# One decoder trunk layer on one core: a wait dropped from SyncE, merge inputs in thirds, four output-weight buffers, experts' second rows in fp32

## The reference, cut to what matters

```python
z = layer_norm(x) @ w_in + b_in                 # queries, keys, values, gates of three token mixers
proj = einsum('blmc,mcd->blmd', branches, w_branch)       # three branches of 256 columns each
y = einsum('blmd,blmd->bld', sigmoid(gates), proj)        # merged by per-channel gates
x = layer_norm(alpha * x + y @ w_out)
h = silu(x @ w_gate[e]) * (x @ w_up[e]) * gate[e]         # 16 experts, each token goes to 2 of them
x = layer_norm(alpha * x + h @ w_down[e])
```

## Time and profile before

| | |
|---|---|
| three runs | 1563.55, 1564.02, 1569.73 us, median 1564.02 |
| the profiled execution | 1564.86 us, span of the trace 1562.8 us |
| PE matmul busy | 1392.9 us, 89% of the span |
| DVE, ACT, POOL busy | 612.7, 489.6, 301.1 us |
| DMA | 228.26 MB, mean 146 GB/s |

### The profile page before, as it was taken

How to read it: one execution, slowest core, us unless ns; L and a number is a source line. 1 busy time by engine, 2 the same in 40 slices (tenths; PEclk the granted TensorE clock), 3 DMA queues, 4 the chain that set the end, 5 groups by cost and what they waited for, 6 DMA issues and landing times. The chain is left out here.

```text
span 1562.8 us, 23344 instructions
## 1 busy us (share of the span) xinstructions
PE 1392.9 (89%) x8799; PEld 1183.2 (76%) x8799; DVE 612.7 (39%) x1598; ACT 489.6 (31%) x904; POOL 301.1 (19%) x406
## 2 busy tenths in 40 slices
PE   4899999999999999878889979969974999999945
PEld 3799999999888989845666646548854888888822
DVE  6122212222324223045676647844551333333317
ACT  4422222222122321136456544320012333333233
POOL 4311140020102000003343100001142222322203
PEclk9799999999999999869999989999986999999967
DMA  7135484163625234580004056732153788887745
GB/s 203 44 119 177 122 234 131 51 164 86 180 62 160 61 84 48 184 222 14 1 1 159 18 193 194 247 101 79 52 170 83 240 270 258 269 272 242 256 174 216
DMA packets 186943, 228.26 MB, mean 146 GB/s; under 512 B 47510, under 2 KB 154902, under 8 KB 185086
## 3 DMA queue, kind: packets, MB, share of 16 engines
q1 hardware_dynamic: 174254, 186.25, 39.0%
q0 software_dynamic: 12592, 40.71, 8.5%
HBM read 167.89 MB, written 60.19 MB: 146 GB/s over the span
## 5 line engine op out<-in xcount | busy, mean ns | idle before, releaser
L1251 PE MATMUL psum<-proj_x_hi,proj_w_hi 128*128 128x362 f32 (+1 forms) x1056 | 357.8, 339 | 8.2 <-DVE proj_w_lo L1373 6.4
L1251 PE MATMUL psum<-proj_x_lo,proj_w_hi 128*128 128x362 f32 (+1 forms) x1056 | 348.9, 330 | 0.0
L1251 PE MATMUL psum<-proj_x_hi,proj_w_lo 128*128 128x362 f32 (+1 forms) x1056 | 348.8, 330 | 0.0
L1251 PEld LDWEIGHTS psum<-proj_x_hi,proj_w_hi 128*128 128x128 f32 x1056 | 201.6, 191 | 13.8 <-DVE proj_w_lo L1373 6.7
L1251 PEld LDWEIGHTS psum<-proj_x_lo,proj_w_hi 128*128 128x128 f32 x1056 | 201.8, 191 | 0.0
L1251 PEld LDWEIGHTS psum<-proj_x_hi,proj_w_lo 128*128 128x128 f32 x1056 | 201.1, 190 | 0.0
L1373 DVE TENSOR_TENSOR proj_w_lo<-proj_w_raw,proj_w_hi 128x1024 fp32r<-128x1024 f32 x44 | 54.2, 1232 | 281.6 <-ACT proj_w_hi L1284 281.5
L1313 ACT ACTIVATE proj_sig<-psum,proj_bias 128x362 f32<-128x362 f32 (+1 forms) x72 | 40.5, 563 | 248.6 <-PE psum L1251 232.8
L2098 PE MATMUL psum<-branches_t,merge_branch_w 128*128 128x362 f32 (+1 forms) x288 | 90.2, 477 | 9.0 <-DMA branches_t<-branch_scratch 9.0
L2552 PE MATMUL psum<-moe_xgt,expert_gate_w 128*128 128x192 f32 x512 | 90.9, 332 | 0.7 <-ACT moe_xgt L2591 0.7
L2552 PEld LDWEIGHTS psum<-moe_xgt,expert_gate_w 128*128 128x128 f32 x512 | 86.8, 195 | 3.2 <-issue 1.1
(11 more groups left out here) (449 smaller groups left out, 2230.1 us busy)
## 6 DMA issues: line engine op xcount, KB each, us to landing
proj_w_raw<-in_w_in SPq DMA_DIRECT2D x43, 512.0 KB, 4.9
expert_gate_w<-in_moe_w_gate SPq DMA_DIRECT2D x16, 1024.0 KB, 9.0
expert_up_w<-in_moe_w_up SPq DMA_DIRECT2D x16, 1024.0 KB, 11.7
expert_down_w<-in_moe_w_down SPq DMA_DIRECT2D x16, 1024.0 KB, 13.6
merge_sig<-gate_scratch SPq DMA_DIRECT2D x24, 544.0 KB, 3.8
gate_scratch<-proj_sig SPq DMA_DIRECT2D x48, 181.0 KB, 1.9
final_pair<-expert_rows SPq DMA_DIRECT2D x8, 1024.0 KB, 11.9
feature_scratch<-proj_feat SPq DMA_DIRECT2D x13, 512.0 KB, 3.0
```

The source lines that it names most:

```text
L1251: mm = nc.tensor.matmul(k.ps[u % RING][:, 0:w], b[wt][:, x % 2, kk, :], b[xx][:, kk, a0:a0 + w], start=(kk == 0 and i == 0), stop=(kk == K ...
```

## The change

1. SP no longer waits for the side outputs at L374; it stores the gates and loads weight tiles on. POOL still waits for them.
2. Each of the three branches is read by three DMAs, one for each token chunk, the first of them ahead of the branch weight. PE waits for the chunk that it uses.
3. The raw buffers for `w_out` become four (`WRAW`). Four tiles are loaded in the merge, one behind the gates of each of the last four units; in the next stage SP has four left.
4. The experts' second 64 rows are four fp32 matmuls on the raw `w_down` and on `hid`, in place of 12 fp32r ones: output columns 0 to 511 go to partitions 0 to 63 of bank 6, columns 512 to 1023 to partitions 64 to 127 of it. ACT copies them in two pieces, `y1_done` counts two for an expert, and `w_down` may be overwritten only after the downs of the expert two before, no longer after its low part is made.

```diff
-        sp.wait_ge(s["side_out"], SIDE_OUT)
...
             for g in range(UNITS):
...
+                if g < 3:
+                    branch(g, 0)
                 sp.dma_start(b["branch_w"][:, g % RING], io["w_branch"][0, m].rearrange("(k p) n -> p k n", p=P)[:, :, dt * P:(dt + 1) * P]).then_inc(s[f"bw_loaded{g % RING}"], 16)
                 if g < 3:
-                    sp.dma_start(br_all[:, 2 * g:2 * g + 2, :], k.br_dram.rearrange("p (c t) -> p c t", c=6)[:, 2 * g:2 * g + 2, :]).then_inc(s[f"br_loaded{g}"], 16)
+                    branch(g, 1)
+                    branch(g, 2)
                 sp.dma_start(b["sig"][:, g % RING, :], k.sig_dram[g]).then_inc(s[f"sig_loaded{g % RING}"], 16)
-            for kk in range(2):
-                load_wo(k, sp, pre, ps, kk)
+                if g >= UNITS - WRAW:
+                    load_wo(k, sp, pre, ps, g - UNITS + WRAW)
...
-            for kk in range(2, KD):
-                sp.wait_ge(s["w_lo_done"], kk - 1)
+            for kk in range(WRAW, KD):
+                sp.wait_ge(s["w_lo_done"], kk - WRAW + 1)
                 load_wo(k, sp, pre, ps, kk)
...
-                        sp.wait_ge(s["wd_lo_done"], g + after("wd_lo_done", -1))
+                        sp.wait_ge(s["down_mm"], g * 2 + after("down_mm", -2))
                         load_down(k, sp, ew, ews, e, x)
...
+                pe.wait_ge(s["y1_done"], g * 2 + after("y1_done", 0))
+                for c in range(2):
                     for half in range(2):
-                        for c in range(2):
-                            for i, (hid, wd) in enumerate((("hid_hi", "wd_hi"), ("hid_lo", "wd_hi"), ("hid_hi", "wd_lo"))):
-                                mm = nc.tensor.matmul(k.ps[4 + 2 * j + half][0:n, :], b[hid][:, c, p0:p0 + n], b[wd][:, x, c, half * 512:(half + 1) * 512],
-                                                      start=(c == 0 and i == 0), stop=(c == 1 and i == 2))
-                    mm.then_inc(s["down_mm"], 1)
+                        mm = nc.tensor.matmul(k.ps[6][64 * half:64 * half + 64, :], b["hid"][:, c, P:CAP], ew["wd"][:, x, c, half * 512:(half + 1) * 512], start=(c == 0), stop=(c == 1))
+                mm.then_inc(s["down_mm"], 1)
...
-                nc.scalar.copy(b["y_out"][0:n, x, 1, :], k.psum[0:n, 6:8, :].rearrange("p b c -> p (b c)")).then_inc(s["y1_done"], 1)
+                for half in range(2):
+                    nc.scalar.copy(b["y_out"][0:n, x, 1, half * 512:(half + 1) * 512], k.ps[6][64 * half:64 * half + n, :]).then_inc(s["y1_done"], 1)
```

## The result

The changed kernel ran in 1540.46 us (median of four, 1538.97 to 1543.79), beside 1563.78 for the kernel before (four runs, 1557.57 to 1569.73). The ratio is 0.9856, interval 0.9831 to 0.9881: faster by 1.4%, 23 us of the 34.7 that were forecast. By the ratio the time is 0.9856 × 1564.02 = 1541.5, half a us above the upper end of the range. The direction was right and the size was not.

A forecast was written before the change was run, and what follows sets the result against it. PE, busy 89% of the span, was taken as the bound: time leaves only where it idles or works in a costlier form. 9.1 + 2.2 + 9.5 + 13.9 = 34.7 off 1564.86 gave 1530 us, range 1525 to 1541.

The forecast's parts named there:

- the halves overlap: Experts' second rows: column halves run side by side, 1.90 us a block; the no-overlap rival had 1555 us, 4%.
- the experts are not held by DMA: Experts: the rival had DMA failing to meet 275 GB/s, period staying 18.18, time 1544 us; 5%.
- `w_down` is not late: Experts: the rival had `w_down` landing 3.1 us late for 14 loads, 43 us lost, time 1573; 3%.
- the third rival: Projection's end: load of tile 42 waits behind the outputs, meets POOL's fetches, lands near 637; time 1539 us; 6%.
- Part 1 (9.1): Projection's end: without SP's wait, 6.38 us of idle PE and 2.72 of slow passes go; lower bound 4.4.
- it will be quicker: Projection's end: load of tile 42 meets a DMA share of 0.05, so lands faster than 11.0 us.
- Part 2 (2.2): Merge start: with branches in thirds PE begins at about 922.3 instead of 924.49; bounds 1.0 and 2.6.
- the last third may land up to a us late: Merge start: thirds issued half a us apart against 1.3 us a chunk on PE; gives the bounds 1.0 and 2.6.
- Part 3 (9.5): Mix: with four raw buffers kk 7 could begin at 1032.5 in place of 1042.36; bounds 8.0 and 9.8.
- Part 4 (13.9): Experts' second rows: 1.90 us in place of 2.77, 0.87 less for each of 16 experts; bounds 16.6 and −11.0.
- The staggered rival: Experts' second rows: passes start strictly in order, five slots, 2.21 us; gain 9.0, time 1535 us; 12%.
- goes against the profiled execution: Whole kernel: gains are subtracted from one profiled execution, 1564.86 us, 0.84 above the runs' median, without correction.

The follow-up runs named there:

- the three sets: Unaltered changed kernel against the kernel before, measured three times: 1540.46, 1533.29 and 1541.25 us, ratios 0.9856, 0.9821 and 0.9841.
- part 4 alone: Kernel before with only the experts' second rows changed to fp32 matmuls: 1554.54 us, ratio 0.9929.
- part 2 alone: Kernel before with only the branches read in thirds: 1564.86 us beside 1565.07, ratio 1.0003.
- part 3 alone: Kernel before with only the four raw buffers and four `w_out` tiles loaded in the merge: 1556.20 us, ratio 0.9946.
- the kernel before in its repeat: Kernel before measured against itself, no code changed: ratio 1.0019 (1.0000 to 1.0038).

## Why the prediction missed, step by step

**The sum of the terms.** The table adds up to −29.7 against −34.7. All four terms were too large: part 2 by 1.6, part 4 by 1.3 (2.4 by its periods), part 3 by 0.8, part 1 by 0.2. And the base was one execution. None of the rivals took the place of the forecast: the halves overlap, the experts are not held by DMA, `w_down` is not late. The load of tile 42 is held behind the outputs, as the third rival had it, but it lands as POOL's fetches begin and does not meet them. By the medians the three sets brought 23.3, 28.7 and 23.3 us; that up to 6 of the 29.7 are not found there stays open. None of the sets reached 1530.

**Part 1 (9.1).** Right in the mean, wrong in the way to it. The step that failed is "it will be quicker": with the engines nearly empty behind the outputs, load 42 was to beat the 11.0 us of before clearly. It landed after 9.9 us, and after 10.2 to 10.6 in the five other profiles with part 1 and the same decode program, each time 0.6 to 1.5 us after POOL's wait for the outputs had ended. The stretch behind the last output, which had a share of 0.05 before, lies 5.6 us later in this execution, and the engines are full there at a low rate (all engines; the last three columns are granted clock, DMA share, GB/s):

```profile
626.00:632.00 6.00, 6.00 (x38) 6.00 (x37) 0.00 (x0) 0.00 (x0) 0.00 (x0) 1.00 0.86 87
```

So dropping SP's wait did not free the load from the outputs; it put the load ahead of POOL's fetches, which start behind the same outputs. That the order in the queue holds it is read from these times and was not tested. I had load 42 at 618 and 43 at 622 to 626; they went at 623.59 and 633.80, since in that execution all of the decode program was 5 us late and the third gate store ahead of load 43 waited, for ACT, which waited for a held gate store (9.64). Both still came in time there: PE waited 0.5 us for the last tile. In the six profiles with part 1 it waited 0.5 to 2.1, so "no PE idle above 1 us" held in three of them. What I also did not see is that the price itself varies: in the five profiles that keep SP's wait PE stood 4.2 to 14.5 us. The longest is that of the kernel with part 4 alone, where SP waited 9.2 us, 0.8 more than in the first profile, and the load took 17.4 us to land beside POOL's fetches, where it took 11.0. That the profile that I summed against lies near their mean (44.5 of 45.5 us for the stage) is luck.

```profile
647.49 0.67 PE L1251 MATMUL psum<-proj_x_hi,proj_w_hi 128*128 128x364 f32 x1 [14.50 <-DVE proj_w_lo L1373]
```

**Part 2 (2.2).** The step that failed is "the last third may land up to a us late", with its lower bound of 1.0. PE did start 1.8 to 2.0 us sooner after the attention, but the next two units' weights and thirds come from the same DMA engines, busy at a share of 1.0 from there on; I had priced the first unit and not the third. Brought 0.6, outside my bounds; it stood in the trace (the third branch landed at 933.3, 10.4 us after its issue, and its unit began at 934.1), and I had not carried it into the sum.

**Part 3 (9.5).** Inside its bounds, 8.7. The landings of the tiles were 3.3 to 5.4 us, median 4.6 instead of the 3.9 that I used, but no wait is left behind the first matmul, so they were not felt. What I had wrong is the pace: I counted 1.39 us for kk 1, and it took 2.56 (1021.20 to 1023.76), because the granted clock was still at its lower level. PE in windows, after:

```profile
1018.50:1023.80 5.30, 5.30 (x13) 0.50 0.79 237
1023.80:1030.00 6.20, 6.20 (x28) 1.00 0.35 138
```

In the other profiles kk 1 took 1.6 to 2.6. The loads beside the merge's end cost nothing, as said.

**Part 4 (13.9).** The step that was mis-sized is the cost of entering and leaving, 0.17 us. The gain for each expert is 18.12 (mean of 14 periods before) − 17.40 = 0.72 instead of 0.87, 11.5 instead of 13.9 (the table's 12.6 has in it what the clock did at the first and last expert; that it lies nearer to 13.9 is luck). The block itself was sized right, 1.87 for 1.90. But I had taken it alone, and its neighbours also pay: the 16 fp32 passes after the block take 2.70 where they took 2.60, and the last fp32r pass before it lasts 0.09 longer until the block. Entering and leaving thus cost 0.34: 0.15 in the block, over four pairs of 0.429, and these 0.19.

The staggered rival needed five slots of 0.429, 2.15 us and more, and 1.87 is below that. I had drawn it from the Trainium skill, "TensorE: Matmul & The Clock Gate", Part 3 on packing small matmuls, which has matmuls start and end strictly in order. That was my reading of it for passes. The trace does not go against the rule for whole matmuls: two passes within 0.01 us of each other are what two matmuls in order, each in its own half, would show; which matmul a pass belongs to the rows do not tell. The period of 19.11 with both halves in the same columns, 0.99 above the 18.12, shows that the whole gain is overlap.

The wait for `w_down` that I priced against a landing of 13.6 us never came near. The median landing fell to 8.5, but only because it is counted from a later issue. Before, the load went out 0.7 us behind the `up` load; now it goes out 6.2 us behind it:

```profile
1301.15 0.53 SPq L2155 DMA_DIRECT2D expert_up_w<-in_moe_w_up  x1
1307.34 0.37 SPq L2159 DMA_DIRECT2D expert_down_w<-in_moe_w_down  x1
```

It lands 14.3 (0.7 + 13.6) and 14.7 (6.2 + 8.5) us after the `up` load's issue, so at the same moment as before. The last stage gave back 0.6, which I have not traced.

**The base.** The largest single piece of the first measurement's shortfall is none of these: 5.2 of the 9.0 us between 34.7 and 25.7 lie before 606 us, where the programs do not differ. The profile before that I summed against had no fall of the clock between 80 and 600 us and one from 635 to 646 (granted clock 0.53 and 0.50 in 635 to 640 and 640 to 645), which part 1 removes; the first profile after had three, which cost 2.5, 1.6 and 1.6 us by the pace of the passes around them, waits taken off. The step of the prediction that failed here is its base: the sum "goes against the profiled execution", as if the stretch ahead of the change cost the same in every execution.

Sorted by the number of such falls, the eleven profiles with the same decode program begin the 985th pass at 620.5 and 621.4 us with none, at 621.0 to 624.1 with one (five profiles), at 624.8 to 626.2 with two (three) and at 626.6 with three. Kernels that keep SP's wait show them as well (part 2 alone near 418 and 513, part 3 alone near 418, part 4 alone near 405, the kernel before in its repeat near 510), one and the same changed program gave 620.5, 622.3 and 626.6, and the means with and without part 1 are 623.8 and 623.3. So nothing says that the change causes them; an effect of a us or two would not show in this spread. That the first set of four runs was slow for this reason is shown for its profiled run alone; for the other three no trace exists, and whether a chip is prone to it stays open.

Three sets give 0.9856, 0.9821 and 0.9841; the kernel before against itself 1.0019. A range of 16 us around a forecast from one execution was too narrow by that spread: by the second and third sets' ratios the time is 1536.0 and 1539.2, inside it, by the first half a us outside.

## What to carry to other kernels

A profiled execution is one draw: before summing against it, look for waits of PE behind which the granted clock stayed full, ask what the same stretch costs when it falls, or take several profiles. An earlier start of a stage that is bound by bytes is worth what its last needed byte moves, and not what its first does. Price another form of matmul by the period of the loop around it, since the neighbours pay part of it. A time to landing counts from the issue: before calling a load fast or slow, look at what stands ahead of it in the queue and when that landed.

## What the runs showed of the hardware that I had not expected

The granted clock fell behind waits of 1.59, 1.83, 2.76, 2.79, 2.86 and 5.15 us in the decode part of the projection, and stayed up behind others of 2.00, 2.15 and 2.53; it also fell between 476 and 500 us in six of the profiles with no wait on PE ahead of it. Behind the wait of 2.0 us near 508, of the same length in eleven profiles, it fell in five and stayed up in six. The length of a wait alone does not tell it. By the marks around them a fall cost 1.2 to 2.5 us. A load of 0.5 MB issued behind nine small outputs took 9.9 to 10.6 us to land, in a stretch with a DMA share of 0.05 without it, and came in just behind those outputs in six of six profiles. And room before the waits, two or three steps of the decode program moved by one projection unit, made the kernel faster than the changed one: 0.9790 (0.9770 to 0.9809) and 0.9774 (0.9748 to 0.9800) of the time before.
